# A delta-rule layer whose projection runs in halves: half product "4" of both pairs as one, in seven quarter products

## What is computed

```python
u = jnp.dot(hmod, w_in)                       # per head: query, key, value, z
qkv, z, b, a = jnp.split(u, ODD_SPLITS, axis=-1)
qkv_c, new_buf = causal_dwconv(qkv, conv_buf, conv_w)   # 4 taps
q, k, v = jnp.split(jax.nn.silu(qkv_c), (GDN_KW, 2 * GDN_KW), axis=-1)
...                                           # q, k normalized; gates beta, g
def step(state, inp):                         # over chunks of 64 tokens
    v_new = u_i - w_i @ state
    o_i = (q_i * exp(g_i)) @ state + qk_i @ v_new
    state = state * exp(g_last) + k_dec.T @ v_new
    return state, o_i
o = rms_norm(o, head_norm) * jax.nn.silu(z)
y = jnp.dot(o, w_out);  x = x + gate * rms_norm(y, norm_post)
```

## Time and profile before

| | us |
|---|---|
| median of 3 runs | 1356.42 |
| lowest, highest | 1355.34, 1356.98 |
| the profiled execution | 1354.85 |
| its span | 1352.7 |
| TensorE busy | 1323.9 (98%) |
| VectorE busy | 806.0 (60%) |
| ScalarE busy | 460.6 (34%) |
| GpSimd busy | 329.4 (24%) |

### The profile page before, as it was taken

The page is one execution under the profiler, slowest core; times in us unless marked ns, Lnnn a source line. Parts: engine busy times, 40 slices in busy tenths (PEclk is TensorE's granted clock), DMA queues, the critical chain, the costliest instruction groups (busy, mean ns, idle before and its releaser), DMA issues.

```text
span 1352.7 us, 27360 instructions
## 1 busy us (share of the span) xinstructions
PE 1323.9 (98%) x11200; PEld 904.0 (67%) x11200; DVE 806.0 (60%) x1866; ACT 460.6 (34%) x1092; POOL 329.4 (24%) x450
## 2 busy tenths in 40 slices
PE   5999999999999999999999999999999999999998
PEld 3577776666654454567877778877888777875543
DVE  4747874455444375674766747657476574772246
ACT  4213442344431232531532514325144251432221
POOL 1023200010013232523312422224222242212352
PEclk9999999999999999999999999999999999999999
DMA  9621007002035422121212112121131211441024
GB/s 368 237 62 36 18 23 278 1 1 79 3 131 184 178 93 100 18 76 25 74 36 68 35 34 86 41 75 36 33 83 31 75 49 33 126 159 27 31 98 169
DMA packets 63296, 111.95 MB, mean 83 GB/s; under 512 B 34778, under 2 KB 38690, under 8 KB 61618
## 3 DMA queue, kind: packets, MB, share of 16 engines
q1 hardware_dynamic: 63172, 110.21, 24.4%
HBM read 91.79 MB, written 18.40 MB: 81 GB/s over the span
## 4 chain that ended last, share of the span: by engine, by line
PE 91%; DVE 5%; DMA 2%; issue 1%; ACT 0%; POOL 0%; SPq 0%; DVEq 0%; POOLq 0%; ACTq 0%
PE psum L1130 87%; PE psum L1133 4%; DMA mem<-modw 2%; DVE mem L2968 1%; DVE mem L3025 0%; DVE mem L3136 0%; DVE mem L2948 0%; DVE mem L3013 0%; DVE mem L3033 0%; DVE mem L3003 0%; DVE mem L3015 0%; DVE mem L3006 0%; DVE mem L3016 0%; DVE mem L3070 0%; DVE mem L3030 0%
## 5 line engine op out<-in xcount | busy, mean ns | idle before, releaser
L1130 PE MATMUL psum<-mem 32*32 32x32 f32 (+12 forms) x10592 | 1261.9, 304 | 6.0 <-DVE mem L2481 1.5
L1130 PEld LDWEIGHTS psum<-mem 128*128 128x128 f32 (+4 forms) x10592 | 835.8, 143 | 400.7 <-issue 215.5
L2968 DVE SCALAR_TENSOR_TENSOR mem<-mem 128x576 f32<-128x576 f32 (+1 forms) x126 | 104.0, 826 | 0.0
L1133 PE MATMUL psum<-mem 128*128 128x128 f32 (+1 forms) x608 | 85.2, 278 | 16.3 <-ACT mem L1925 12.5
L1133 PEld LDWEIGHTS psum<-mem 128*128 128x128 f32 (+1 forms) x608 | 70.7, 144 | 40.7 <-issue 20.1
L2277 ACT ACTIVATE mem<-mem 128x128 f32<-128x128 f32 x72 | 22.1, 307 | 123.7 <-DVE mem L3180 70.5
L2160 ACT ACTIVATE mem<-psum 128x288 f32<-128x288 f32 x28 | 11.5, 412 | 108.7 <-PE psum L1130 108.7
L1009 POOL COPY mem<-mem 128x3 f32<-128x3 f32 x24 | 8.4, 350 | 148.8 <-DVE mem L2926 69.9
L2054 ACT ACTIVATE mem<-mem 128x256 f32<-128x256 f32 x72 | 35.5, 494 | 26.4 <-DVE mem L2703 26.4
L2170 ACT ACTIVATE mem<-mem 128x576 f32<-128x576 f32 (+1 forms) x42 | 32.7, 779 | 27.3 <-DVE mem L2946 27.3
L983 POOL TENSOR_TENSOR mem<-mem 128x512 f32<-128x512 f32 x14 | 15.3, 1091 | 107.7 <-issue 93.3
(11 more groups left out here) (259 smaller groups left out, 1275.5 us busy)
## 6 DMA issues: line engine op xcount, KB each, us to landing
mem<-modw SPq DMA_DIRECT2D x12, 2048.0 KB, 11.8
mem<-w SPq DMA_DIRECT2D x44, 512.0 KB, 4.4
mem<-x SPq DMA_DIRECT2D x10, 512.0 KB, 4.6
x_dram<-mem SPq DMA_DIRECT2D x9, 512.0 KB, 2.9
mem<-row_dram SPq DMA_DIRECT2D x8, 576.0 KB, 5.5
mem<-x_dram SPq DMA_DIRECT2D x9, 512.0 KB, 3.7
mem<-wout SPq DMA_DIRECT2D x1, 4096.0 KB, 15.3
mem<-gs SPq DMA_DIRECT2D x8, 512.0 KB, 3.6
```

The lines of the kernel that those rows point to most:

```text
L1130: return pe.matmul(*a, **k)
L1133: return pe.transpose(out, in_, ident[0:n, 0:n])
L2968: x = dve.scalar_tensor_tensor(cvm, U1[:, m, lo + j:hi + j], CW[:, 3 * g + ORDER[m], j:j + 1], cvm, ALU.mult, ALU.add)
```

## The change

**One half product for both pairs.** Half product "4" multiplies the lower half of each pair's second weight block with TD4, the same tokens for both pairs. The results of the two pairs are now taken as one 2 x 2 problem: the two weight blocks side by side (JA, JB) against TD4 cut into four quarters (QX11 to QX22), and this problem again by the same method, in seven products `SUBS` of half the depth (2 tiles) instead of 2 x 2 x 4 = 16 products: 14. A head has 110 products instead of 112; slots 10 and 11 hold one less each. All parts now stand in one list, `PARTS`, and a part's PSUM bank is its index modulo 2, with waits for the additions and copies of the part two before it (`bank_left`, `free_bank`).

**What that needs.** GpSimd makes four 128 x 256 sums a head (`both_sums`) ahead of `head_sums(h + 1, 1)`, and in head 0 four differences of quarters (`quarter_diffs`, 128 x 576 each) behind TD4; both TD4 and these now stand before the copies L1034 to L1038. They lie in the room of `gate`, which is stored to DRAM before the heads, loaded again in head 6, and waited for by VectorE before its first use behind the last head. ScalarE copies two quarter products out (`second_pair`), VectorE adds five, and one new addition `s21` (128 x 576) joins pair 1's scratch to the value buffer behind step "6" of pair 1.

**Orders.** Pair 0 runs "1675", then the seven quarter products, then "2", "3"; pair 1 runs "1", "6", "5", "7", "2", "3". With that the parts close in other slots: pair 1's "6" closes in slots 29 and 30 (before 26 and 27), "5" in 31 and 33 (before 31 and 33 too, its first half in 31), "7" in 34 and 35 (before 29 and 30); pair 0's "3" closes in 23 and 25 (before 21 and 22). The taps of key and query move from the slots 18 to 31 to the slots 20 to 31; slots 28 and 30 get one. SP's reload in head 6 goes in the order "6", "5", "7", and `w1out[2]` waits for "7" in place of "4".

**The scan.** On VectorE the sample-state addition at k = 6 moves from before the copy of VN to behind it.

```diff
-SLOTS = ([3, 3, 3, 3, 3, 3, 3, 3] + [3] + [2, 3] + [3, 3]
+SLOTS = ([3, 3, 3, 3, 3, 3, 3, 3] + [3] + [2, 2] + [2, 3]
...
+SUBS = ("1", "2", "6", "5", "7", "3", "4")
+PARTS = ([(0, s, j) for s in "1675" for j in range(2)] + [(BOTH, "4", s) for s in SUBS]
+         + [(0, s, j) for s in "23" for j in range(2)]
+         + [(1, s, j) for s in "165723" for j in range(2)])
...
-TAP = {18: (KEY, 0, 1), 19: (KEY, 0, 2), 20: (KEY, 0, 3), 21: (KEY, 1, 1), 22: (KEY, 1, 2), 23: (KEY, 1, 3),
-       24: (QUERY, 0, 1), 25: (QUERY, 0, 2), 26: (QUERY, 0, 3), 27: (QUERY, 1, 1), 29: (QUERY, 1, 2), 31: (QUERY, 1, 3),
+TAP = {20: (KEY, 0, 1), 21: (KEY, 0, 2), 22: (KEY, 0, 3), 23: (KEY, 1, 1), 24: (KEY, 1, 2), 25: (KEY, 1, 3),
+       26: (QUERY, 0, 1), 27: (QUERY, 0, 2), 28: (QUERY, 0, 3), 29: (QUERY, 1, 1), 30: (QUERY, 1, 2), 31: (QUERY, 1, 3),
...
+            sp.dma_start(gate_dram, gate).then_inc(sem("x1_out1"), 16)
...
+                    if ahead == 1:
+                        sp.dma_start(gate, gate_dram).then_inc(sem("modb_in"), 16)
...
-                    for i, step in enumerate(("6", "7", "5")):
+                    for i, step in ((0, "6"), (2, "5"), (1, "7")):
                         sp.wait_ge(sem("st_mm"), passed(h + 1, 1, step))
...
+            def both_sums(g):
...
+                pool.tensor_tensor(JS3, JA[:, low], JB[:, low], ALU.subtract).then_inc(sem("s_made"), 1)
+                pool.tensor_tensor(JS1, JB[:, low], JB[:, high], ALU.add).then_inc(sem("s_made"), 1)
+                wait(pool, sem("s_made"), weights_summed(g, BOTH, "s1"))
+                pool.tensor_tensor(JS2, JS1, JA[:, low], ALU.subtract).then_inc(sem("s_made"), 1)
+                wait(pool, sem("s_made"), weights_summed(g, BOTH, "s2"))
+                pool.tensor_tensor(JS4, JA[:, high], JS2, ALU.subtract).then_inc(sem("s_made"), 1)
+
+            def quarter_diffs():
...
+                pool.tensor_tensor(QT3, QX22, QX12, ALU.subtract).then_inc(sem("t_ready"), 1)
...
+                pool.tensor_tensor(QX12, QX12, QX11, ALU.subtract).then_inc(sem("t_ready"), 1)
...
+                pool.tensor_tensor(QT2, QX22, QX12, ALU.subtract).then_inc(sem("t_ready"), 1)
...
+                pool.tensor_tensor(QT4, QX21, QT2, ALU.subtract).then_inc(sem("t_ready"), 1)
...
+                if h == 0:
+                    wait(pool, sem("pj_mm"), 12)
+                    wait(pool, sem("t_ready"), DIFF0 + DIFF["t2"])
+                    pool.tensor_tensor(TD4, halves(1, 0), TD2, ALU.subtract).then_inc(sem("t_ready"), 1)
+                    quarter_diffs()
                 wait(pool, sem("n_ev1"), 7 * h + 5)
                 pool.tensor_copy(XW[0:32, :, 0:32], XT0[0:32, 0:NT - 1])
...
                 if ahead:
+                    both_sums(h + 1)
                     head_sums(h + 1, 1)
...
+                    if (q, j) == (1, 1):
+                        dve.wait_ge(sem("st_add"), summed(g, 1, "6", "u2"))
+                        dve.wait_ge(sem("st_cp"), evicted(g, BOTH, "4", "4"))
+                        v = U1[:, VALUE, PRE:PRE + LO]
+                        dve.tensor_tensor(v, v, UD.rearrange("p j u -> p (j u)"), ALU.add).then_inc(sem("st_add"), 1)
...
-                        if k == 6:
-                            dve.wait_ge(sem("sample_mm"), 4 * h + SAMPLE_MM["kv"])
-                            dve.wait_ge(sem("ss_dec"), h + 1)
-                            ss = SS1.rearrange("p (b s) v -> p b (s v)", b=4)
-                            dve.tensor_tensor(ss, ss, psum[:, 2:6, 0:256], ALU.add).then_inc(sem("sample_dve"), 1)
                     dve.wait_ge(sem("tr_mm"), 8 * h + k + 1)
                     dve.tensor_copy(VN, at_(6, 1)).then_inc(sem("vn_ready"), 1)
...
+                    elif k == 6:
+                        dve.wait_ge(sem("sample_mm"), 4 * h + SAMPLE_MM["kv"])
+                        dve.wait_ge(sem("ss_dec"), h + 1)
+                        ss = SS1.rearrange("p (b s) v -> p b (s v)", b=4)
+                        dve.tensor_tensor(ss, ss, psum[:, 2:6, 0:256], ALU.add).then_inc(sem("sample_dve"), 1)
                     between(h, 13 + 3 * k, ahead)
...
+            dve.wait_ge(sem("modb_in"), 48)
             partial(0)
```

More of the change, by code:

```diff
@@ L136, in out_added, with passed, summed, evicted @@
     return len(OUT_ADDS) * p + OUT_ADDS[name]
[L139 to L151, removed]
+def passed(g, q, step, at=1):
+    return MM0 + len(PARTS) * (g - 1) + PARTS.index((q, step, at)) + 1
+def summed(g, q, step, name, at=1):
+    return ADD0 + len(ADDED) * (g - 1) + ADDED.index((q, step, at, name)) + 1
+def evicted(g, q, step, at):
+    return CP0 + len(COPIED) * (g - 1) + COPIED.index((q, step, at)) + 1
+def weights_summed(g, q, name):
+    return SUM0 + len(PER_HEAD_SUMS) * (g - 1) + PER_HEAD_SUMS.index((q, name)) + 1
+def half_bank(g, i):
+    return (len(PARTS) * (g - 1) + i) % 2
+def bank_left(g, i):
+    i -= 2
+    if i < 0:
+        g, i = g - 1, i + len(PARTS)
+    before = PARTS[:i + 1]
+    return (ADD0 + len(ADDED) * (g - 1) + sum(a[:3] in before for a in ADDED),
+            CP0 + len(COPIED) * (g - 1) + sum(part in before for part in COPIED))
 def z_count(h, n):
@@ L464, in encoder @@
         UD = take(2, SUB)
+        JS = take(3, HALF // 2, P)
+        gate_flat = gate.rearrange("p w d -> p (w d)")
+        QT3, QT2, QT4 = (gate_flat[:, i * HALF // 2 * SUB:(i + 1) * HALF // 2 * SUB]
+                         .rearrange("p (k u) -> p k u", u=SUB) for i in range(3))
+        JS3, JS1, JS2 = (JS[:, i] for i in range(3))
+        JS4 = gate_flat[:, 3 * HALF // 2 * SUB:3 * HALF // 2 * SUB + HALF // 2 * P].rearrange("p (k c) -> p k c", c=P)
         assert at[0] <= ARENA - 2 * D
@@ L939, in head_sums @@
                     wait(pool, sem(f"w1_in{m}"), 16 * g + 16)
-                n = SUM0 + 4 * pair_of(g, q)
                 if (g, q) != (1, 0):
@@ L1523, in product, with free_bank, half_product @@
                     x.then_inc(sem("pj_mm"), 1)
-            def half_product(g, u, k):
-                q, i = divmod(u, STEPS)
-                step, j = PASSES[i // 2], i % 2
+            def free_bank(g, i):
+                if g == 1 and i < 2:
+                    pe.wait_ge(sem("z_ev"), 2 + i)
+                    return
+                adds, copies = bank_left(g, i)
+                pe.wait_ge(sem("st_add"), adds)
+                pe.wait_ge(sem("st_cp"), copies)
+            def half_product(g, i, k):
+                q, step, j = PARTS[i]
+                if q == BOTH:
+                    both_product(g, i, k)
+                    return
@@ L2213, in between @@
                     leave(GROUPS - 1)
-                for dh, u in closed(p):
-                    if PASSES[u % STEPS // 2] == "1" and (ahead or not dh):
-                        first_pass(h + dh, u // STEPS, u % 2)
+                for dh, i in closed(p):
+                    q, step, j = PARTS[i]
+                    if ahead or not dh:
+                        if q != BOTH and step == "1":
+                            first_pass(h + dh, q, j)
+                        elif q == BOTH and j in ("5", "4"):
+                            second_pair(h + dh, j)
                 if ahead and p in FIRST_TAP:
@@ new lines, in added_half @@
+                    dve.tensor_tensor(UD[:, j], c11, p, ALU.add).then_inc(sem("st_add"), 1)
+                    if (q, j) == (1, 1):
[3 more added lines that the diff above has]
+                        dve.tensor_tensor(v, v, UD.rearrange("p j u -> p (j u)"), ALU.add).then_inc(sem("st_add"), 1)
+                    return
+                if step == "7" and q == 0:
+                    dve.wait_ge(sem("st_add"), summed(g, 0, "6", "u2", j))
+                    dve.wait_ge(sem("s1_ready"), 3 * (g - 1) + KEY + 1)
+                    x = dve.tensor_tensor(c21, UD[:, j], p, ALU.add)
```

232 lines of the change are left out of this document (148 added, 84 removed).

## The result

The kernel with the change takes 1371.14 us (median; 1369.06 to 1371.9), the kernel before 1356.2 beside it: a ratio of 1.0111, 95% interval 1.0098 to 1.0123, 15 us slower. The profiled execution of after took 1371.9, with a span of 1370.1 against 1352.7.

A forecast was written before the change was run, and what follows sets the result against it. TensorE, busy 98%, was taken as the bound, with VectorE bounding head starts. Terms -6.8 + 6.2 + 1.9 + 7.2 + 2.7 = +11.2 gave 1366.05 profiled, 1367.6 as median; own range 1360 to 1373, wider 1357 to 1375.

The forecast's parts named there:

- Two products less: TensorE, slots 10 and 11 of seven heads: two half products fewer at 0.483 us each, -6.8 us.
- Scan step 6: VectorE's 128x576 sum and a tap ahead of the copy delay TensorE 0.89 us a head, +6.2 (4.9 to 7.0).
- the 0.6 named as its sign: At scan step 6 TensorE waits 0.6 us or more for VectorE's sample-state addition in every head but the last.
- Scan step 4: VectorE's add closing in slot 23 delays the instruction TensorE waits on: 0.27 us a head, +1.9 (0.7 to 2.6).
- A head's end: GpSimd's three late weight sums hold off VectorE's front: 1.2 us at each of six transitions, +7.2 (0 to 9.9).
- the second meeting: At a head's end L3013 meets GpSimd's third sum, waiting as long as L3007 (0.6 to 0.7), less about 0.2.
- SP's queue: Head 6's reload waits for step "7", delaying the last output weights up to 4.55 us: +2.7 once (0 to 3.5).
- Head 0 and the rest: GpSimd's differences ahead of head 0's block copies, small sums, ScalarE copies, gate transfers and bank waits: 0, range to 1.5.
- A: Rival, chance 0.17: step "7"'s lateness is hidden at heads' ends and on SP's queue; not slower, 1357.7 us.
- B: Rival, chance 0.10: scan step 6 is hidden as well, leaving -4.9 us; faster, 1351.5 us.
- C: Rival, chance 0.08: GpSimd's 1.04 us power of the norms also holds VectorE off, 6.2 us more; 1373.8 us.

The follow-up runs named there:

- the last run: Kernel after with early sums, reload last and the 128x576 sum in halves, plus slot 23's addition carried out in slot 24: 1349.22 us, ratio 0.9951.
- run 4: Kernel after with the sample-state addition at scan step 6 put back ahead of the copy of the new value: 1375.63 us, ratio 1.0143.
- run 2: Kernel before with one edit, GpSimd's three sums of the next-but-one head's first weights waiting for step 4 instead of 7: 1365.74 us, ratio 1.0072.
- run 5: Kernel after with the last two rows' reload in head 6 moved on SP's queue behind the next head's state load: 1365.73 us, ratio 1.0072.
- runs 1, 3 and 4: Kernel after, each with one edit: two of GpSimd's three sums freed early (1363.12 us); 128x576 sum moved behind copy and sample-state addition (1369.17 us); run 4.
- runs 5 to 8: Run 5; then cumulatively on the kernel after: early sums with reload last (1356.76 us), the 128x576 sum in halves (1351.65 us), and the last run.

## Why the prediction was right, and where it was off

The predicted time was 1367.6 with a range of 1357 to 1375; 1371.1 lies in it, on the forecast side, 3.5 above. A head's period, forecast at 86.5, is 86.8 us. Step by step:

- **Two products less**, -6.8: right. It is hidden in after, and comes out in the last run (-6.4).
- **Scan step 6**, 0.89 a head: 0.87, of which 0.29 at the copy. The sum was priced at 0.72 between an add and a tap; it holds VectorE 0.67 (842.50 to 843.17). The sum in halves gives 5.1 back, the term was 6.2. The wait for the addition shows as 0.42, below the 0.6 named as its sign, because the products ahead of it are late already. That the move of the addition is no loss here was in the sum only implicitly; run 4 shows it.
- **Scan step 4**, 0.27 a head: 0.27 by the starts in head 2 (TensorE's step to the waiting product is 0.59 us instead of 0.32), and 2.4 us by the last run against 1.9.
- **A head's end**, 1.2 a transition, at most 1.65: mis-sized; 1.53 on the mean in the trace, 9.2 for the six transitions, 10.0 by run 2, against 7.2. The mechanism and the first victim (L3007) were right, and so was that victim's price: 0.62 more in the median of L3162, against 0.6 to 0.7. The step that failed is the second meeting. The prediction counted only instructions with two inputs in SBUF and let the third sum meet L3013. L3009, with one input and 0.17 us long, stands ahead of it: it met the third sum and waited for its whole rest, which cost 0.95, so nothing was saved by alternating. The prediction also looked for the lateness at L3136 alone; two thirds of it is met earlier, at the bank wait for L3083, which does not change the sum, since what is waited for there is not waited for again.
- **SP's queue**, 2.7: mis-sized; 5.4 by run 5. The shift was right in kind, but two things came with it. The store behind the reload, 4.4 us late by run 5 (4.55 forecast), took 8.2 us until the state load went out (6.4 in run 5), and the last weights went out 6.5 later than there. And behind the standstill TensorE ran at its lower clock for some 3 us, worth 1.7, for which the sum had no term.
- **Head 0 and the rest**, 0: right as far as shown; TensorE's products wait for no copy of GpSimd's in head 0 (its weight loads do once, 0.5).

The two terms that were off lie 2.0 (9.2 against 7.2) and 2.7 (5.4 against 2.7) above their sizes, both the same way; the median is 3.5 above the forecast. The wait of 1.5 us put down to "issue", which the sum did not have, is within the second. In the two traces the parts add up to the whole: -6.8 for the products, +6.1 and +1.9 for the scan, +9.2 for the heads' ends, +5.8 for the last head from its start on (157.3 against 151.5), and +1.3 for the "issue" wait, which swallows the 0.24 at head 7's start: 17.5, where the spans are 17.4 apart. The medians are 14.9 apart, because the profiled execution of after is 0.8 above its median and that of before 1.35 below its own; why these executions differ from the others of their kernel stays open.

Of the rivals, A (the lateness hidden) and B (step 6 hidden) fall with the waits above. C, the norms' power beside L3015, falls too: GpSimd's L1139 runs 858.19 to 859.3 in after, and L3170, with both inputs in SBUF, starts under it and takes 0.46, as its forerunner L3015 did before; L3168, begun just ahead of it, takes 0.48. By the Trainium skill ("SBUF — State Buffer", "Who interferes with whom") the shared ports are held for the whole instruction; the trace agrees for the 128x512 sums, to within 0.3 us of their ends, and disagrees for the power. The price that the prediction worked out by this rule for the sums, near 1.5 a transition, is what they cost (1.53); the 1.2 that went into its forecast allowed for alternating.

Open: the 1.5 us of "issue" at head 6's end. It comes and goes with the reload's place on SP's queue (1.5 us in runs 1, 3 and 4, which leave it where it is in after; runs 5 to 8, which move it, have no such wait there). What it waited for is not shown.

## What to carry to other kernels

A change that saves work on the bounding engine is worth its saving only if every wait that closed earlier still does: list what each moved release frees on the other engines (here a buffer for GpSimd and a queue position for SP), and where that work lands then. Price a meeting of GpSimd and VectorE by the whole rest of GpSimd's instruction, and not only for VectorE instructions with two inputs in SBUF: here a short one with one input waited just as long. Of a buffer that is freed late, ask which of the results really need it: here one of three, and it could be worked out later from another of them and a block of weights still in place.

## What the runs showed of the hardware that was not expected

- A VectorE instruction of 0.17 us with one input in SBUF (TENSOR_SCALAR, 128x9) took 1.12 when GpSimd's 128x512 sum was ahead of it, in after and in run 2; a TENSOR_REDUCE of one input (L3161, 854.78) beside the second sum kept its 0.45. The Trainium skill ("SBUF — State Buffer", "Who interferes with whom") says as much of both: it counts tensor_scalar among the operations that can take the shared ports, tensor_reduce on this chip among those that never do. Read for L3009 ahead of the prediction, it would have pointed at the second meeting.
- GpSimd's power (L1139, 1.13 us) did not hold off the VectorE instruction that started under it (L3170, two inputs in SBUF, 0.46).
- A standstill of 4.24 us on TensorE was followed by about 3 us at TensorE's lower clock (granted 0.62 on the mean of 1224 to 1227), and by the full clock from 1227 on; in run 5, without the standstill, the lower clock does not appear.
